# Conditioning products of a decoder step: the nine vectors move through resident weight blocks

## The reference

```python
def adaln(c, w, b, n):
    m = jax.nn.silu(c) @ w + b
    return jnp.split(m[:, None, :], n, axis=-1)

def modulate(h, shift, scale):
    return h * (1.0 + scale) + shift

sh1, sc1, g1, sh2, sc2, g2 = adaln(c, p['w_mod'][l], p['b_mod'][l], 6)
h = modulate(rmsnorm(x, p['g_mix'][l]), sh1, sc1)
```

## Time and profile before

| | us |
|---|---|
| median of 3 runs | 2092.38 |
| lowest, highest | 2089.8, 2096.78 |
| span of the profiled execution | 2097.7 |
| TensorE busy (its weight loads) | 1912.2 (986.0) |
| VectorE, ScalarE, GpSimd busy | 524.1, 331.0, 142.7 |

### The profile page before, as it was taken

How to read it: one execution, slowest core, us unless ns; L and a number is a source line. 1 busy time by engine, 2 the same in 40 slices (tenths; PEclk the granted TensorE clock), 3 DMA queues, 4 the chain that set the end, 5 groups by cost and what they waited for, 6 DMA issues and landing times.

```text
span 2097.7 us, 20023 instructions
## 1 busy us (share of the span) xinstructions
PE 1912.2 (91%) x6138; PEld 986.0 (47%) x6138; DVE 524.1 (25%) x1090; ACT 331.0 (16%) x669; POOL 142.7 (7%) x272
## 2 busy tenths in 40 slices
PE   7989999999889689999997897898987789999995
PEld 3456666444466344444444674232325444444444
DVE  0021002222310311111111205777762211111112
ACT  0000001222200111111111101112120111111111
POOL 3300000111100000000000000011110000000000
PEclk9989999999989659999998896677789569999997
DMA  9745332677435019999995233566652029999972
GB/s 361 272 167 200 144 138 80 233 265 276 168 141 208 12 40 327 350 355 346 349 347 209 93 143 127 201 235 242 233 194 97 0 102 349 348 348 351 348 275 82
DMA packets 84607, 459.10 MB, mean 219 GB/s; under 512 B 10392, under 2 KB 11560, under 8 KB 46032
## 3 DMA queue, kind: packets, MB, share of 16 engines
q1 hardware_dynamic: 52560, 347.56, 46.3%
q0 software_dynamic: 30944, 105.53, 13.5%
q10 hardware_dynamic: 1056, 5.36, 0.6%
HBM read 402.72 MB, written 55.69 MB: 219 GB/s over the span
## 4 chain that ended last, share of the span: by engine, by line
PE 86%; DVE 8%; DMA 2%; issue 2%; ACT 1%; DVEq 0%; SPq 0%; POOLq 0%; ACTq 0%
PE bank L694 84%; DVE arena L1859 1%; PE bank L706 1%; DVE h L1855 1%; DMA y_rows<-arena 1%; PE bank L1007 1%; DMA ring<-wstream 1%; ACT xn L1268 0%; DVE xn L1482 0%; DVE rstd L1480 0%; PE bank L708 0%; DVE h L1491 0%; DVE arena L1575 0%; DMA arena<-y_rows 0%; ACT arena L1247 0%
## 5 line engine op out<-in xcount | busy, mean ns | idle before, releaser
L694 PE MATMUL bank<-ring,arena 128*128 128x512 f32 (+2 forms) x1728 | 718.6, 573 | 11.6 <-DVE arena L1721 11.6
L694 PEld LDWEIGHTS bank<-ring,arena 128*128 128x128 f32 (+1 forms) x1728 | 318.7, 188 | 364.9 <-issue 354.8
L694 PE MATMUL bank<-arena 128*16 128x512 f32 (+7 forms) x992 | 422.2, 574 | 37.9 <-DMA arena<-y_rows 19.9
L1247 ACT ACTIVATE arena<-bank 128x256 f32<-128x256 f32 (+8 forms) x334 | 143.1, 442 | 1005.8 <-PE bank L694 838.3
L694 PEld LDWEIGHTS bank<-arena 128*128 128x128 f32 (+5 forms) x992 | 162.5, 186 | 253.7 <-issue 209.0
L694 PE MATMUL bank<-ring,cs 128*9 128x256 f32 x896 | 206.7, 384 | 11.2 <-DMA ring<-wstream 10.8
L694 PE MATMUL bank<-h,ring 128*128 128x264 f32 x640 | 151.5, 395 | 8.0 <-DVE h L1493 8.0
L694 PEld LDWEIGHTS bank<-h,ring 128*128 128x128 f32 x640 | 121.4, 193 | 41.3 <-issue 13.0
L694 PEld LDWEIGHTS bank<-ring,cs 128*9 128x9 f32 x896 | 78.0, 92 | 130.8 <-issue 33.8
L694 PE MATMUL bank<-arena,ring 128*128 128x264 f32 x512 | 119.4, 395 | 13.9 <-DVE arena L1579 13.0
L1738 DVE TENSOR_TENSOR arena<-bank,arena 128x256 f32<-128x256 f32 x64 | 27.1, 424 | 412.6 <-ACT arena L1355 412.6
(11 more groups left out here) (207 smaller groups left out, 876.3 us busy)
## 6 DMA issues: line engine op xcount, KB each, us to landing
ring<-wstream SPq DMA_DIRECT2D x296, 1024.0 KB, 7.1
arena<-vcache POOLq DMA_DIRECT2D x64, 512.0 KB, 5.2
y_rows<-arena POOLq DMA_DIRECT2D x64, 512.0 KB, 9.2
arena<-kcache SPq DMA_DIRECT2D x64, 512.0 KB, 4.7
arena<-state POOLq DMA_DIRECT2D x32, 512.0 KB, 6.8
ss_out<-arena POOLq DMA_DIRECT2D x32, 512.0 KB, 5.6
arena<-y_rows POOLq DMA_DIRECT2D x8, 512.0 KB, 5.0
sp_out<-arena ACTq DMA_DIRECT2D x4, 512.0 KB, 2.8
```

Of the source, the lines that this page charges most:

```text
L694: ins = nc.tensor.matmul(out, w, rhs, start=start, stop=stop, skip_group_check=True)
L1247: return nc.scalar.activation(out, in_, ACT.Copy)
```

## The change

The sides of the conditioning products are exchanged. `mod_columns` makes, for each of a slot's two tiles of 128 outputs, 8 accumulated products with the 128 x 128 weight block as the stationary side and the nine columns of `cs` moving; the result is nine columns that go straight to their place in the collecting bank. A slot is now 16 products instead of 8. `mod_rows` on both engines, `mod_turn`, the tile `mrow` and the banks of the rows are gone; the bias add on VectorE is as before. In the first stage the collecting bank is taken at the head of a lap instead of after its first slot. In the gates a slot's halves are now its two tiles instead of its two groups of row blocks.

```diff
 def plan_turns():
     t = Turns()
-    t.loop(24 // R, [(("row0", r), (X1, X2)[r % 2]) for r in range(R)] + [("mod0", M)])
+    t.loop(24 // R, [("mod0", M)])
...
-            def mod_rows(key, n, it=None, blocks=range(KT)):
+            def mod_columns(ps, tile, n, tiles=range(2), done=None):
 
                 w = slot(n)
-                b, _ = turn(key, it)
-                ps, full = begin(key, it) if blocks[0] == 0 else (bank[b], filled[b])
-                for k in blocks:
-                    mm(ps[0:NC, 0:256], cs[:, k, :], w[:, k, :], k == 0, k == KT - 1,
-                       full if k == KT - 1 else None)
-
-            def mod_turn(key, buf, ps, tile, done=None, it=None):
-
-                moved(pe, key, it)
-                for m in range(2):
-                    turned(ps[:, (tile + m) * NC:(tile + m + 1) * NC], mrow[0:NC, buf, m * P:(m + 1) * P], NC,
-                           m == 0, done if m else None)
+                for m in tiles:
+                    out = ps[:, (tile + m) * NC:(tile + m + 1) * NC]
+                    for k in range(KT):
+                        mm(out, w[:, k, m * P:(m + 1) * P], cs[:, k, :], k == 0, k == KT - 1,
+                           done if m * k == KT - 1 else None)
...
             def mod0_lap(it):
+                ps, full = begin("mod0", it)
                 for r in range(R):
                     pe.wait_ge(slot_in[r], it * 16 + 16)
                     first_of_slot[0] = not (isinstance(it, int) and r == 0)
-                    mod_rows(("row0", r), r, it)
-                    if r == 0 and isinstance(it, int):
-                        pe.wait_ge(consts_in, 48)
-                    if r == 0:
-                        ps, full = begin("mod0", it)
-                    else:
-                        mod_turn(("row0", r - 1), (r - 1) % 2, ps, 2 * (r - 1), None, it)
-                mod_turn(("row0", R - 1), (R - 1) % 2, ps, 2 * (R - 1), full, it)
+                    mod_columns(ps, 2 * r, r, range(2), full if r == R - 1 else None)
...
                 take_slot(n + 1)
-                mod_rows(("row1", 16 + i), n + 1, None, range(0, 4))
+                mod_columns(mod1_ps, 32 + 2 * i, n + 1, range(1))
                 read_state(4 * i + 2)
                 value_rows(4 * i + 3)
-                mod_rows(("row1", 16 + i), n + 1, None, range(4, 8))
-                mod1_turn(15 + i)
+                mod_columns(mod1_ps, 32 + 2 * i, n + 1, range(1, 2), mod1_full if i == 7 else None)
                 read_state(4 * i + 3)
-            mod1_turn(23)
...
-            with act.Fori(0, 24 // R) as it:
-                for r in range(R):
-                    mod_rows(("row0", r), r % 2, it)
-
```

More of the change, by code:

```diff
@@ L131, in plan_turns @@
     t.add("past_total", X0)
-    for i in range(16):
-        t.add(("row1", i), X2)
     for h in range(RH):
@@ L145, in plan_turns @@
             t.add(("g", i, m), L[(2 * i + m) % 4])
-        t.add(("row1", 16 + i), X2)
     for h in range(RH):
@@ L152, in plan_turns @@
     t.add("kvmod", M)
-    for i in range(8):
-        t.add(("row2", i), X2)
     for n in range(4):
@@ L304, in build @@
         vrow = xn[0:NS].rearrange("p a b -> p (a b)")[:, 0:RH * RV]
-        mrow = ret.take(2, 256)
         qz = ret.take(2, RH, NS * NS)
@@ L784, in mod1_slot @@
                 take_slot(S_RET + 2 * i + 1)
[L785 to L790, removed]
+                mod_columns(mod1_ps, 2 * i, S_RET + 2 * i + 1)
             def values(key, skey, n, src, i):
@@ L946, in _ @@
                     i = 2 * n + half
[L947 to L950, removed]
+                    mod_columns(kv_ps, 2 * i, j + 1, range(2), kv_full if i == 7 else None)
             def moe(l, base):
@@ L1253, in _ @@
             eps = c_("eps")
-            def mod_rows(key, buf, it=None):
-                ps = result(act, key, it)
-                copy(mrow[0:NC, buf, :], ps[0:NC, 0:256]).then_inc(free(key), 1)
-            with act.Fori(0, 24 // R) as it:
-                for r in range(R):
-                    mod_rows(("row0", r), r % 2, it)
             def rms(r):
@@ L1274, in _ @@
             for i in range(8):
-                mod_rows(("row1", i), i % 2)
-            for i in range(8):
                 for c in range(2):
@@ L1279, in _ @@
                     copy(vtok[:, c, i * 256:(i + 1) * 256], ps[:, 0:256]).then_inc(free(("v", i, c)), 1)
-                mod_rows(("row1", 8 + i), i % 2)
             for hd in range(RH):
@@ L1304, in _ @@
                         .then_inc(free(("g", i, m)), 1)
-                mod_rows(("row1", 16 + i), i % 2)
                 if i % 2:
@@ L1318, in _ @@
                     .then_inc(free(("gn", hd)), 1)
-            for i in range(8):
-                mod_rows(("row2", i), i % 2)
             def moe(l):
```

## The result

| | us |
|---|---|
| before, median of 4 runs | 2094.58 (2089.8 to 2098.24) |
| after, median of 4 runs | 2211.9 (2203.41 to 2219.89) |
| ratio | 1.0563, 95% interval 1.0531 to 1.0595 |
| span of the profiled execution, before and after | 2097.7, 2201.9 |

The profiled execution of after is the shortest of its four, 2203.4 us; its span is 104.2 us longer than that of before.

A forecast was written before the change was run, and what follows sets the result against it. TensorE, busy 91% of the span, was taken to bound the kernel. Terms 66 + 57 + 2 - 1 = +124 us, added to 2097.7 less 5.3, gave 2216 us, likely range 2178 to 2253.

The forecast's parts named there:

- What one slot costs: Conditioning slot on TensorE: 32 records set by the weight load, 3.52 us at full clock, 6.88 us at half.
- The clock of the first stage: First conditioning stage: clock stays at half throughout, first sum starts at 175.9 instead of 110.61; term +66 us.
- The 0.6 us wait at the head of a lap: First stage: TensorE waits for VectorE's bias add of the lap before, about 0.6 us at three lap heads, 1.8 us.
- the saved wait for ScalarE: End of first stage: ScalarE's square no longer queues behind its copies, which had cost TensorE 1.41 us.
- one row of three: Profile rows at 112 to 115, 1275 to 1280 and 717 to 768 us, read as thin work failing to keep full clock.
- The mixed stages: Query and key, values, gates, output projection: 470.5 us at full clock, divided by mean clock 0.865, gives 543.9, +57 us.
- The price at the full clock: Four mixed stages at full clock: 470.5 us against 487.0, -16.5 us; gates 184.5 against 186.1.
- What is left: Remaining effects: heads and head norms +2 us, earlier next sum after the projection -1 us, weight stream not in the way.
- The +2 for the heads and the head norms: Retention heads and head norms: same work, but a few microseconds at half clock after a narrow block, +2 us.
- The difference of 5.3 us: Whole kernel: median of runs taken as 5.3 us below the profiled span of 2097.7 us, subtracted from the forecast.
- That the clock would hold everywhere: Rival for the whole kernel: gapless stream keeps full clock everywhere, -33 us, 2059 us; chance 0.07.
- That it would hold in the mixed stages: Rival: half clock only in the first stage, full clock in the mixed stages, +47 us, 2139 us; chance 0.05.

The follow-up runs named there:

- the mixed order: Against the changed kernel, each narrow product of query and key, values and output projection placed behind a wide one, same instructions otherwise: 2203.5 us.
- the best kernel: The changed kernel with 126 moving columns in all conditioning products, padded sort and value rows padded to 128 rows: 2016.4 us, 0.9626 of the kernel before.

## Why the prediction was right, step by step

**What one slot costs** held: 3.52 us at the full clock was foreseen, 3.49 measured; 6.88 at half, 6.86 measured. The load sets the step: nine and 63 columns take the same 41.1 and 41.2 us a lap. With 126 moving columns a record takes 0.113 us (21.70 / 192) against 0.109 with nine, both at the full clock.

**The clock of the first stage** held. Foreseen was a start of the first sum at 175.9, measured 174.83. The 0.6 us wait at the head of a lap and the saved wait for ScalarE came as written. The forecast rested on one row of three: from 717 to 768 PE had no idle time, but in 1275 to 1280 it was busy for only 3.72 of 5 us, and 112 to 115 came behind a wait, so these two could not tell a thin stream from a gap. The columns as the cause were shown only by the runs with 126. The check I had named for it, a granted clock of 0.50 in that window, was a bad one, since the view cannot show it there; the pace, 6.9 us a slot, was the good one.

**The mixed stages** were right in kind and off in size. The four windows have 0.91, 0.94, 0.83 and 0.87, inside the 0.81 to 0.93 that I held for likely but for the values; the sum, from 490.3 to 534.5 us, is +44 in this execution, the shortest of the four, where the term was +57. The mis-sized step is the one mean of 0.865 for all four. By it the gates were to grow by 27 us and the other three by 30; they grew by 34 and 10. In query and key a fall costs little, since the wide products behind it bring the clock back soon (211.71 and 225.16 are partly slow, 238.12 is not); the gates have value rows of 8 rows next to the narrow blocks, and with these rows padded they stay at 1.00. The price at the full clock was off too: the gates were to win 1.6 us, and with 126 columns they take 188.0 against 187.9. I had noted that rows of 8 partitions count for little, for the sort, and did not look for them in the gates.

**What is left** had one gain not foreseen: the sum of squares ahead of the experts ran at a fuller clock than before (3.81 us for 5.48), and from its first product to the sort it took 34.8 us instead of 38.7. The +2 for the heads and the head norms came to +0.4.

**The difference of 5.3 us** between span and median, which I carried along, was an accident: the profiled execution of before, with a span of 2097.7 us, was among its longest, and that of after was the shortest of its four. So part of the closeness is luck. The terms came to +104 where I had +124, 20 too many; the median of after lies 10.0 us above its span where I had put it 5.3 below, 15 too few. The two misses leave 4 us. The medians differ by 117.

**The rivals.** That the clock would hold everywhere gave 2059 us; the kernel with 126 columns, in which it does hold, took 2072, so that price was right to 13 us and only its condition was not met. That it would hold in the mixed stages gave 2139; with 126 columns there it took 2148. By the Trainium skill (TensorE: Matmul & The Clock Gate, section Why this matters for your kernels) a TensorE that is kept busy keeps the upper clock. The trace does not agree for this thin stream: TensorE had no idle gap for 41 us at a time and stayed at half.

## What to carry to other kernels

Before exchanging the sides of a product, price the new form at both levels of the clock and ask what the array will see: many rows and many moving columns, or a thin stream. Where a weight load sets the pace anyway, moving more columns, even copies, was nearly free here (0.113 for 0.109 us a record) and paid for the clock; padding products of 8 rows to 128 paid too. And read the clock from the pace of equal records, above all ahead of the first change that the trace shows.

## What the runs showed that I had not expected

- Holding and raising the clock seem to be different things. In the mixed order a stage that began cold stayed at 0.50 for 28.5 us and then stayed up with the same products; why it rose when it did is open. With 63 columns the first stage stayed at half for 168 us, while the mixed stages, which have wide products too, were at 0.97 to 1.00.
- Much of the spread between executions seems to come from the gates. After ranges over 16.5 us, the kernel that is narrow in the gates alone over 14.0; with 126 columns in the gates alone, the narrow products elsewhere left in place, it is 3.2. These are 4, 10 and 4 runs, and the kernel before, whose gates are at 1.00, ranges over 14.9 us in the 13 runs beside the last of these, so the gates are not the only source. Why one execution has more falls than another was not tried; that the clock's changes fall differently against the instructions each time is only argued.
- In the best kernel the padding of the sort and of the value rows, which has nothing to do with the change, is worth 56 us (2072.2 to 2016.4), more than the 21 us that the change is worth when it is made with 126 columns (2092.8 before, in the same comparison). The kernel before was not run with these paddings, so what the change is worth beside them is open.
